# Residual kept in SBUF past the token norm, head 1's weights by slot, last head's states stored by ScalarE, low-rank columns beside head 0's values

## The chip, the cores and the metric

The kernel runs on one core of one Trainium2 chip. The metric is the device time of one execution in microseconds. All arithmetic is in fp32. "Record" below is one instruction in the trace; an fp32 matmul of the program makes two of them on TensorE (PE).

## The reference, cut to what matters

Two layers of a streaming encoder over 1024 prompt frames and 32 sample frames (NTOK = 1056 rows of D = 1024 features), with 256 memory rows:

```
h = rms_norm(x, g0)                                  # layer 0
u, a, b, zA, qB, kB, vB, zB = split(h @ W0)
o_A = gated_deltanet(silu(causal_conv(u)), a, b)     # 8 heads, 128x128 states
o_B = band_attention(qB, kB, vB)                     # 16 heads of 64
x += concat(rms_norm(o_A) * silu(zA), o_B * silu(zB)) @ Wout0
x += memory_attend(rms_norm(x), keys/values from rms_norm(mem))
h = rms_norm(x, g1)                                  # layer 1
q, k, v, lr, z = split(h @ W1)                       # lr has 16 columns
lg = log_sigmoid(lr @ W_gate_up + gate_bias) / 16
x += (rms_norm(gla(q, k, v, lg)) * silu(z)) @ Wout1
x += memory_attend(rms_norm(x), ...)
```

Outputs are x, the new states of both recurrences, the last convolution rows and the keys and values. The memory's keys and values of both layers are computed inside the GDN part.

## The kernel before, in words

The program is a series of stages, each with blocks in which the five engines run their own lists of instructions. A block ends when all engines have ended their lists, and the next begins after a barrier (recorded at L45, or at a block's own line such as L1834). Features lie on the 128 partitions: `hT` holds the normed input as 8 slabs of 128 features by 1056 tokens. `Wb` holds four weight slots of 1024x128. A projection of one head is cut into **jobs**: 352 tokens by 8 slabs, 16 records at L490 (GDN) or L1995 (GLA).

`turn_input` (L86 to L198) makes `hT`. For each of 9 tiles of 128 tokens (the last has 32) PE transposes the rows into PSUM (`turn_TP`, L138), ScalarE (ACT) copies them to `xT` (L160) and squares them into `sq` (L162), PE sums the squares with a matrix of ones (L128), ACT makes the reciprocal root, and VectorE (DVE) multiplies by gain and root into `hT`, 8 instructions per tile (L185). SyncE's queue (SP) loads the rows, the gain `g` (L115) and GDN's first weights (L59), then stores `xT` to `x_features` tile by tile (L119) and waits for these stores before the block ends. The residual is read back from `x_features` much later.

`gdn` (L205): PE's order at its start is head 0's first 3 jobs, gate columns (L675), 6 jobs, transposes of memory tile 0 (`turn_mem`, L668), 3 jobs, memory tile 1, then 36 transposes of 8 columns (L693, "tok"), then `head(0)`: 12 steps of head 1's projection as filler (24 records, L490) and the turn of conv k (L546). DVE copies tok (L1082), makes the decay differences (L903), prepares the parameters, and runs conv k and conv q (L938, L941), before which it copies the convolution's tails (L931, L932) and for that waits for the head's last projection copy (`proj_out` 12). ACT applies SiLU to conv k (L759, L760). SP loads head h+1's four weight slots in `head(h)`; for head 0 this stands after the wait for the stores of the turned memory (`m_st`), L364. After the last head SP loads band's first weights (L59, slots in the order of `ahead`), stores the last head's state, sample state and output rows (L372 to L387) and waits for them.

`band` (L1230) projects k first; PE and ACT wait at the start for constants (`consts`, two memsets of `Qz` by DVE, L1756). `EARLY_ORDER` and `BAND_COL` say which weight slot holds what.

`gla` (L1808) opens with a block of its own (L1834 to L1865): weights `wlr` of the 16 low-rank columns are loaded, PE multiplies them with `hT` (L1849), DVE copies the result to `lrT`, SP waits for the parameters. Then the main block starts: z0, z1, v, q, k of head 0 (`PLAN`), with 9 tiles of v at 256 columns (L1991).

Of the kernel before, what the change touches and what calls it, by code (L numbers as in the profile page):

```python
# [6 lines left out]
F32 = mybir.dt.float32  # L7
ACT = mybir.ActivationFunctionType
ALU = mybir.AluOpType
# [76 lines left out]
def turn_input(nc, ident, ones, eps, x_in, xT_dram, gain, hT, ahead):  # L86

    with ExitStack() as ctx:
        def sb(n, shape):
# [5 lines left out]
        xT = sb("xT", [128, KD, NTOK])  # L95
# [7 lines left out]
        turned, copied, squared, summed, rooted, rs_ok, h_out, st = (sem("turned"), sem("copied"), sem("squared"), sem("summed"),  # L103
                                                                     sem("rooted"), sem("rs_ok"), sem("h_out"), sem("st"))
# [4 lines left out]
        with nc.Block() as block:  # L109
            @block.sync  # L110
            def _(sp):
# [3 lines left out]
                sp.dma_start(g[:, :], gain.rearrange("(k p) -> p k", p=128), allow_slow_non_contiguous=True).then_inc(g_ld, 16)  # L115
# [29 lines left out]
            def _(act):  # L145
                act.preload_act_table_set("natural_log_exp_and_others")
# [10 lines left out]
                for t in range(TILES):  # L157
# [3 lines left out]
                    wait(act, summed, t - 1)  # L161
                    act.activation(sq[:, t % 2, :, 0:r], TP[:, t % 2, :, 0:r], ACT.Square).then_inc(squared, 1)  # L162
# [5 lines left out]
            def _(pool):  # L168
# [3 lines left out]
                                   base=0, pattern=[[-1, 128]], channel_multiplier=1).then_inc(ident_ok, 1)  # L172

# [31 lines left out]
def gdn(nc, ident, ones, eps, hT, W, w_ld, w_in, conv_w, conv_state, a_log, dt_bias, onorm_g, state_in,  # L205
        gate_rows, o_dram, conv_p, conv_s, state_p, state_s, mem, mem_layers, mem_T, ahead):
# [3 lines left out]
    with ExitStack() as ctx:  # L210
# [36 lines left out]
        OI = sb("OI", [128, TILES, 128])  # L247
# [112 lines left out]
        with nc.Block() as block:  # L360
            @block.sync
            def _(sp):
# [26 lines left out]
                def head(h, before):  # L389

                    for p, j in enumerate(ORDER):

                        sp.wait_ge(proj_done, h * 12 + 3 * p + 3)
                        load_w(h + 1, j, h * 128 + 128 + COL[j])
# [2745 lines left out]
```

## Time and profile before

| | |
|---|---|
| median of 3 runs | 3653.94 us (3649.12 to 3654.18) |
| the profiled execution | 3648.23 us, span 3646.5 us |
| mean granted TensorE clock | 0.985 |
| PE busy | 3506.4 us, 96% of the span |
| DVE, ACT, POOL busy | 1169.9, 1102.5, 514.8 us |
| read and written in HBM | 158.49 and 45.99 MB |

The span is the time from the first to the last instruction. A row of the timeline is a run of like instructions on one engine, with its start in us from the span's start, its length, their count, and in brackets the idle time ahead of it with what ended it. SPq is SP's list of DMA issues. A row of stretches gives busy time per engine and PEclk, the share of TensorE's full clock that was granted.

### The profile page before, as it was taken

The numbers are of one execution on the slowest core, as the hardware profiler recorded it, in microseconds if no ns is written. First come the engines' busy times: TensorE is split into PE (matmuls) and PEld (weight loads), VectorE is DVE, ScalarE is ACT, GpSimd is POOL, SyncE is SP. The second block draws the span as 40 slices with busy tenths as digits, with TensorE's granted clock in tenths as the row PEclk, the third lists the DMA queues.
The fourth block names the chain that finished last, engine by engine and source line by source line (L and its number), as shares of the span: only waits on it lengthen the run. The fifth ranks groups of instructions, "written<-read, shape, count | busy, mean of one in ns | idle before, by whom it ended". The sixth has DMA issues, their size and how long they took to land. (4 is left out here: it accounts for less than half of the span.)

```text
span 3646.5 us, 47398 instructions
## 1 busy us (share of the span) xinstructions
PE 3506.4 (96%) x16670; PEld 2579.1 (71%) x16670; DVE 1169.9 (32%) x2993; ACT 1102.5 (30%) x2794; POOL 514.8 (14%) x518
## 2 busy tenths in 40 slices
PE   7899999999799999999999998999999999899999
PEld 5577777777468777777766675677777777566676
DVE  2355555555213333333320234022221122220223
ACT  3333333333133443443310242022222222210242
POOL 0344444444000000000001002000000000011000
PEclk9899999999899999999999999999999999999999
DMA  5211311102412231222261102111111111371101
GB/s 138 64 32 32 26 35 31 37 26 94 95 42 45 40 31 42 45 46 82 96 196 47 35 10 75 41 29 39 50 44 43 29 43 38 109 234 46 35 1 48
DMA packets 254233, 206.85 MB, mean 57 GB/s; under 512 B 21071, under 2 KB 232175, under 8 KB 254039
## 3 DMA queue, kind: packets, MB, share of 16 engines
q1 hardware_dynamic: 249726, 194.83, 21.0%
q10 hardware_dynamic: 4320, 9.67, 0.7%
q8 instruction: 100, 1.64, 0.2%
q14 instruction: 87, 0.71, 0.1%
HBM read 158.49 MB, written 45.99 MB: 56 GB/s over the span
## 5 line engine op out<-in xcount | busy, mean ns | idle before, releaser
L490 PE MATMUL gdn_pj<-hT,Wb 128*128 128x352 f32 x1536 | 517.8, 463 | 28.8 <-PEq L45 15.8
L1995 PE MATMUL gla_pj<-hT,Wb 128*128 128x352 f32 x1536 | 470.0, 460 | 2.2 <-PEq L1834 1.6
L1426 PE MATMUL band_pj<-hT,Wb 128*128 128x384 f32 (+1 forms) x1152 | 385.1, 464 | 23.2 <-DVE band_tick L1761 20.2
L1995 PEld LDWEIGHTS gla_pj<-hT,Wb 128*128 128x128 f32 x1536 | 290.7, 190 | 151.0 <-issue 2.9
L490 PEld LDWEIGHTS gdn_pj<-hT,Wb 128*128 128x128 f32 x1536 | 267.6, 193 | 118.5 <-issue 32.6
L1426 PEld LDWEIGHTS band_pj<-hT,Wb 128*128 128x128 f32 x1152 | 206.6, 192 | 105.0 <-DVE band_tick L1761 20.5
L1991 PE MATMUL gla_pj<-gla_Wv,hT 128*128 128x256 f32 x1152 | 264.9, 379 | 0.0
L1991 PEld LDWEIGHTS gla_pj<-gla_Wv,hT 128*128 128x128 f32 x1152 | 217.7, 190 | 29.5
L1611 ACT ACTIVATE band_E<-band_NS,band_nm 128x576 f32<-128x576 f32 (+9 forms) x136 | 89.7, 660 | 213.8 <-DVE band_nm L1688 213.7
L1189 POOL TENSOR_TENSOR gdn_BT<-gdn_AT,gdn_level 128x384 f32<-128x384 f32 x144 | 143.8, 1029 | 35.3 <-DVE gdn_TT L972 17.9
L1456 PE MATMUL band_pj<-Wb,hT 128*128 128x128 f32 x1152 | 144.2, 276 | 0.0
L1519 PEld LDWEIGHTS band_PX<-band_ET,band_VT 128*128 128x128 f32 x976 | 127.1, 192 | 20.2
L1456 PEld LDWEIGHTS band_pj<-Wb,hT 128*128 128x128 f32 x1152 | 136.6, 192 | 0.7
L1519 PE MATMUL band_PX<-band_ET,band_VT 128*128 128x128 f32 x976 | 131.0, 275 | 0.0
L1688 DVE CUSTOM_DVE_ANT_0 band_NS<-band_SC,band_bias 128x576 f32<-128x576 f32 (+9 forms) x136 | 83.2, 611 | 138.8 <-issue 138.0
L2685 PE MATMUL fin_ps<-fin_R,fin_Wx 128*128 128x384 f32 (+1 forms) x384 | 123.1, 463 | 2.2 <-DVE fin_xT L2976 2.1
L2676 PE MATMUL fin_ps<-hT,Wb 128*128 128x384 f32 (+1 forms) x384 | 124.9, 460 | 0.0
L1489 PE MATMUL band_SC<-band_KN,band_Qz 128*128 128x288 f32 (+3 forms) x448 | 114.9, 374 | 3.5 <-issue 3.5
L2649 PE MATMUL fin_ps<-hT,fin_Wq 128*128 128x384 f32 (+1 forms) x384 | 117.2, 460 | 0.0
L2617 PE MATMUL fin_ps<-hT,Wb 128*128 128x384 f32 (+1 forms) x384 | 115.9, 460 | 0.0
L1621 ACT ACTIVATE band_ET<-band_PT 128x512 f32<-128x512 f32 (+3 forms) x136 | 70.7, 520 | 148.9 <-PE band_PX L1499 89.7
L2939 DVE TENSOR_TENSOR fin_xT<-fin_xT,fin_ps 128x384 f32<-128x384 f32 (+1 forms) x48 | 24.8, 521 | 279.3 <-PE fin_ps L2617 244.0
(412 smaller groups left out, 5419.3 us busy)
## 6 DMA issues: line engine op xcount, KB each, us to landing
Wb<-in_l_w_in_dram SPq DMA_DIRECT2D x96, 512.0 KB, 6.2
fin_xT<-x_features SPq DMA_DIRECT2D x16, 528.0 KB, 7.4
fin_R<-o_features SPq DMA_DIRECT2D x16, 528.0 KB, 9.7
Wb<-in_l_w_mkv_dram SPq DMA_DIRECT2D x8, 1024.0 KB, 5.5
Wb<-in_l_w_out_dram SPq DMA_DIRECT2D x16, 512.0 KB, 4.2
gla_Wv<-in_l_w_in_dram SPq DMA_DIRECT2D x8, 1024.0 KB, 5.2
o_features<-gla_OF ACTq DMA_DIRECT2D x14, 528.0 KB, 5.7
gdn_GB<-gate_rows SPq DMA_DIRECT2D x8, 544.0 KB, 3.6
```

The costliest lines, as they stand in the source:

```text
L490: mm = pe.matmul(pj[:, m % 2, 0:w], W[:, j, k, :], hT[:, k, c0:c0 + w], start=k == 0, stop=k == KD - 1)
L1189: pool.tensor_tensor(g3(BT, g), g3(AT, g), mask, ALU.mult).then_inc(masked, 1)
L1426: mm = pe.matmul(out[:, 0:w], W[:, j, k, :], hT[:, k, c0:c0 + w], start=k == 0, stop=k == KD - 1)
L1456: mm = pe.matmul(out[:, 0:128], hT[:, k, 128 * i:128 * i + 128], W[:, 3, k, :], start=k == 0, stop=k == KD - 1)
L1489: mm = pe.matmul(out[:, b, 0:w], q, KN[p][:, k0 + w * b:k0 + w * b + w], start=True, stop=True)
L1519: mm = pe.matmul(PX[:, 1, :], v, ET[:, u % 2, 128 * b:128 * b + 128], start=b == 0, stop=b == blocks(u) - 1)
L1991: mm = pe.matmul(pj[:, m % 2, 0:DV_C], hT[:, k, 128 * x:128 * x + 128], Wv[:, k, :], start=k == 0, stop=k == KD - 1)
L1995: mm = pe.matmul(pj[:, m % 2, 0:w], W[:, SLOT[kind], k, :], hT[:, k, c0:c0 + w], start=k == 0, stop=k == KD - 1)
L2617: mm = pe.matmul(ps[:, 3 * (n % 2) + c, 0:w], weights, src[:, c0:c0 + w], start=i == 0, stop=i == len(tiles) - 1)
L2649: mm = pe.matmul(ps[:, i % 3, 0:w], Wqt[:, h, k, :], hT[:, k, c0:c0 + w], start=k == 0, stop=k == KD - 1)
L2676: mm = pe.matmul(out[:, 0:w], Wz[:, x, k, :], hT[:, k, c0:c0 + w], start=k == 0, stop=k == KD - 1)
L2685: mm = pe.matmul(out[:, 0:w], Wo[:, k, 128 * x:128 * x + 128], O[:, k, c0:c0 + w], start=k == 0, stop=k == M_H - 1)
```

## The change

In `turn_input` `xT` becomes `x_kept`, a tile that lives through `gdn`; its nine stores and the wait for them are gone. The gain is loaded by ACT's queue. The squares are made by GpSimd (POOL) from SBUF, and PE's transposes wait for the copy and no longer for the square.

```diff
-                for t in range(TILES):
-                    sp.wait_ge(copied, t + 1)
-                    sp.dma_start(xT_dram.rearrange("(k p) t -> p k t", p=128)[:, :, cols(t)], xT[:, :, cols(t)]).then_inc(st, 16)
-                sp.wait_ge(st, TILES * 16)
...
-                    wait(pe, squared, t - 1)
+                    wait(pe, copied, t - 1)
...
+                act.dma_start(g[:, :], gain.rearrange("(k p) -> p k", p=128), allow_slow_non_contiguous=True).then_inc(g_ld, 16)
...
-                    act.activation(sq[:, t % 2, :, 0:r], TP[:, t % 2, :, 0:r], ACT.Square).then_inc(squared, 1)
...
+                    pool.tensor_tensor(sq[:, t % 2, :, 0:rows(t)], xT[:, :, cols(t)], xT[:, :, cols(t)], ALU.mult).then_inc(squared, 1)
```

In `gdn` SP stores `x_kept` as eight DMAs at the start; `dec`, `TM`, `BT`, `VV`, `KR`, `KE`, `OI` and `zs` become slices of `x_kept`, so ACT and DVE wait for `x_st` before they first write there. Head 1's weights are loaded one slot at a time (`next_w`). The memory transposes use two PSUM banks, and PE's order is changed. Conv k waits for `proj_out` 9, and the two tail copies stand between conv k and conv q.

```diff
+                for k in range(KD):
+                    sp.dma_start(xT_dram[128 * k:128 * k + 128, :], xT[:, k, 0:NTOK]).then_inc(x_st, 16)
                 sp.dma_start(sall[:, :, :], state_in.rearrange("h d v -> d h v")).then_inc(ld_state, 16)
+                next_w(0, 0)
+                next_w(0, 1)
...
-                        wait(pe, m_ok, 4 * m + 2 * r)
+                        wait(pe, m_ok, 2 * (2 * m + r - 1))
...
-                            mm = pe.transpose(X3[:, 2, 128 * k:128 * k + 128], M[m][:, c:c + 128], ident[:, :])
+                            mm = pe.transpose(X3[:, 2 - r, 128 * k:128 * k + 128], M[m][:, c:c + 128], ident[:, :])
...
+                act.wait_ge(x_st, KD * 16)
...
-                    dve.wait_ge(proj_out, h * 12 + 12)
...
+                    dve.wait_ge(proj_out, h * 12 + 9)
...
+                        if x == 1:
+                            wait(dve, v_turn, h * 4)
+                            dve.wait_ge(proj_out, h * 12 + 12)
```

At the end of `gdn` ACT issues the last head's four stores, output columns 0 to 767 as soon as they are ready; SP no longer does. Band's weights sit in other slots (`BAND_SLOT`), k's and q's are loaded first, and `EARLY_ORDER` follows. In `band` PE waits for `consts` after the k jobs, ACT before the first q norm.

```diff
-                        load_ahead(sp, [ahead[j] for j in ((2, 3) if x == 6 else (0, 1))])
+                        load_ahead(sp, [ahead[j] for j in ((0, 1) if x == 6 else (2, 3))])
...
-                store_state(H_A - 1)
-                store_out(H_A - 1)
...
+                act.wait_ge(s_ok, H_A * N)
+                act.dma_start(state_p[last:H_A, :, :].rearrange("o d v -> d (o v)"), S[:, 0, :]).then_inc(st_p, 16)
+                act.dma_start(state_s[last:H_A, :, :].rearrange("o d v -> d (o v)"), Sn[:, :]).then_inc(st_s, 16)
+                act.wait_ge(o_fin, last * 3 + 2)
+                act.dma_start(o_dram[128 * last:128 * H_A, 0:768], OF[:, 0:768]).then_inc(st_o, 16)
...
-BAND_COL = [4112, 5136, 7184, 6160]
...
+BAND_SLOT = [2, 3, 0, 1]
...
-                pe.wait_ge(consts, 2)
-                for _ in stream(0, 0):
-                    pass
+                for m, _ in enumerate(stream(0, 0)):
+                    if m + 1 == ends[place["k", 0]]:
+                        pe.wait_ge(consts, 2)
```

In `gla` the opening block is gone. The 16 low-rank columns are appended to head 0's v weights, whose 9 tiles become 272 columns wide; ACT copies them apart (9 small copies), PE transposes them (`turn_lr`, 9 transposes) after z1, and DVE makes `lrT`. Head 0's order is z0, v, z1, q, k.

```diff
-                            mm = pe.matmul(pl[:, c, 0:w], wlr[:, k, :], hT[:, k, c0:c0 + w], start=k == 0, stop=k == KD - 1)
...
+        Wv = sb("Wv", [128, KD, DV_C + RANK])
...
+        PLAN0 = PLAN[0:3] + PLAN[6:15] + PLAN[3:6] + PLAN[15:]
...
+                sp.dma_start(Wv[:, :, DV_C:DV_C + RANK], w_cols[:, :, COL["lr"]:COL["lr"] + RANK]).then_inc(lr_ld, 16)
...
+                            act.activation(lr[:, x, :], pj[:, m % 2, DV_C:DV_C + RANK], ACT.Copy)
```

How the instructions move, at three places. PE's list at the start of `gdn` (`gdn_AT` and `gdn_QK` are the two memory tiles, `gdn_WQ`, `gdn_EG`, `gdn_OF` the rows of tok, the last x12 the head start's filler); a count here is of the program's matmuls, two records each, before:

```order
24 L490 MATMUL gdn_pj<-hT,Wb 128x352 x48
25 L668 MATMUL gdn_X<-ident,gdn_AT 128x128 x8
26 L490 MATMUL gdn_pj<-hT,Wb 128x352 x24
27 L668 MATMUL gdn_X<-ident,gdn_QK 128x128 x8
28 L693 MATMUL gdn_X<-ident,gdn_WQ 128x8 x18
29 L693 MATMUL gdn_X<-ident,gdn_EG 128x8 x9
30 L693 MATMUL gdn_X<-ident,gdn_OF 128x8 x9
31 L490 MATMUL gdn_pj<-hT,Wb 128x352 x12
32 L546 MATMUL gdn_X<-ident,gdn_act 128x128 x9
```

and in the change:

```order
24 L497 MATMUL gdn_pj<-hT,Wb 128x352 x48
25 L675 MATMUL gdn_X<-ident,gdn_AT 128x128 x8
26 L497 MATMUL gdn_pj<-hT,Wb 128x352 x8
27 L675 MATMUL gdn_X<-ident,gdn_QK 128x128 x8
28 L497 MATMUL gdn_pj<-hT,Wb 128x352 x8
29 L701 MATMUL gdn_X<-ident,gdn_WQ 128x8 x18
30 L701 MATMUL gdn_X<-ident,gdn_EG 128x8 x9
31 L701 MATMUL gdn_X<-ident,gdn_OF 128x8 x9
32 L497 MATMUL gdn_pj<-hT,Wb 128x352 x20
33 L553 MATMUL gdn_X<-ident,gdn_act 128x128 x9
```

One job now stands between the memory tiles, one between tile 1 and tok, and one joins the filler behind tok. SP's queue at the same place (`Wb` there is head 1's weights), before:

```order
18 L416 DMA gdn_sall<-in_state_l_gdn_dram 128x8x128
19 L418 DMA gate_rows<-gdn_WQ 8x1152
20 L367 DMA gdn_GB<-gate_rows 128x1088
21 L425 DMA mem_features<-gdn_BT 128x8x128
22 L425 DMA mem_features<-gdn_VV 128x8x128
23 L425 DMA mem_features<-gdn_KR 128x8x128
24 L425 DMA mem_features<-gdn_KE 128x8x128
25 L364 DMA Wb<-in_l_w_in_dram 128x8x128 x4
```

and in the change:

```order
15 L420 DMA x_features<-x_kept 128x1056 x8
16 L421 DMA gdn_sall<-in_state_l_gdn_dram 128x8x128
17 L361 DMA Wb<-in_l_w_in_dram 128x8x128 x2
18 L425 DMA gate_rows<-gdn_WQ 8x1152
19 L364 DMA gdn_GB<-gate_rows 128x1088
20 L361 DMA Wb<-in_l_w_in_dram 128x8x128
21 L433 DMA mem_features<-x_kept 128x8x128 x4
22 L361 DMA Wb<-in_l_w_in_dram 128x8x128
```

Three of head 1's four slots are now issued ahead of the memory's stores. SP's queue at the end of `gdn` (`gdn_S`, `gdn_Sn` the states, `gdn_OF` the output rows, `band_rel` band's first load), before:

```order
93 L458 DMA out_dram<-gdn_U 128x512 x2
94 L59 DMA Wb<-in_l_w_in_dram 128x8x128 x2
95 L372 DMA out_dram<-gdn_S 128x128
96 L373 DMA out_dram<-gdn_Sn 128x128
97 L386 DMA o_features<-gdn_OF 128x1024
98 L387 DMA o_features<-gdn_OF 128x32
99 L360 UNCONDITIONAL_BRANCH
100 L1331 UNCONDITIONAL_BRANCH
101 L1379 DMA band_rel<-in_l_b_rel_bias_dram 16x257
```

and in the change:

```order
90 L467 DMA out_dram<-gdn_U 128x512 x2
91 L59 DMA Wb<-in_l_w_in_dram 128x8x128 x2
92 L357 UNCONDITIONAL_BRANCH
93 L1354 UNCONDITIONAL_BRANCH
94 L1402 DMA band_rel<-in_l_b_rel_bias_dram 16x257
```

The four stores have gone to ACT's list, behind its last instruction there.

## Rows read from the trace of the kernel before

**Rows 1.** The page's part 1, busy us and share of the span

```profile
PE 3506.4 (96%) x16670; PEld 2579.1 (71%) x16670; DVE 1169.9 (32%) x2993; ACT 1102.5 (30%) x2794; POOL 514.8 (14%) x518
```

**Rows 2.** What PE waited for, whole run: us in total, times, longest

```profile
PE gdn_X L546 <- ACT gdn_act L760: 7.4, 6, 1.5
```

**Rows 3.** PE timeline, input stage: start, us, line, out<-in, xcount, [idle before <-releaser]

```profile
16.65 1.95 PE L128 MATMUL turn_PS<-turn_sq,ones 128*128 128x128 f32 x16
...
48.03 16.31 PE L490 MATMUL gdn_pj<-hT,Wb 128*128 128x352 f32 x48 [15.79 <-PEq L45]
```

**Rows 4.** DVE and SP's queue, timeline, input stage

```profile
15.70 12.69 DVE L185 SCALAR_TENSOR_TENSOR hT<-turn_xT,turn_g,turn_rs 128x128 f32<-128x128 f32 x48 [13.80 <-DMA turn_g<-in_l_norm_g_dram]
...
31.38 3.49 DVE L185 SCALAR_TENSOR_TENSOR hT<-turn_xT,turn_g,turn_rs 128x128 f32<-128x128 f32 x16 [0.37 <-ACT turn_rs L154]
...
21.44 21.98 SPq L119 DMA_DIRECT2D x_features<-turn_xT  x9
```

**Rows 5.** DVE and POOL timelines, GLA around 2397, GDN at 99.61

```profile
2397.68 2.00 DVE L2246 TENSOR_TENSOR gla_KK<-gla_raw,gla_E 128x32 f32<-128x32 f32 x1
...
2396.71 2.92 POOL L2320 TENSOR_TENSOR gla_QS<-gla_QG,gla_FC 128x1088 f32<-128x1088 f32 x1 [106.98 <-DVE gla_QG L2243]
...
99.61 2.11 POOL L1154 TENSOR_TENSOR gdn_conv<-gdn_conv,gdn_tap 128x1091 f32<-128x1091 f32 x1
```

**Rows 6.** Stretches: us, busy PE, PEld, DVE, ACT, POOL, PEclk, DMA, GB/s

```profile
36.00:40.00 4.00, 0.00 (x0) 0.00 (x0) 0.00 (x0) 0.00 (x0) 0.00 (x0) 0.50 1.06 297
```

**Rows 7.** PE timeline, start of GDN

```profile
108.84 0.60 PE L668 MATMUL gdn_X<-ident,gdn_AT 128*128 128x128 f32 x4
...
111.42 14.37 PE L490 MATMUL gdn_pj<-hT,Wb 128*128 128x352 f32 x48
...
129.74 0.94 PE L693 MATMUL gdn_X<-ident,gdn_WQ 8*128 8x8 f32 x15 [1.47 <-DVE gdn_KE L1076]
...
145.50 9.96 PE L490 MATMUL gdn_pj<-hT,Wb 128*128 128x352 f32 x24 [12.98 <-issue]
```

**Rows 8.** DVE, ACT and SP's queue, timeline, start of GDN

```profile
90.60 1.06 ACT L864 ACTIVATE gdn_BT<-gdn_AT 128x1024 f32<-128x1024 f32 x1
...
132.55 0.28 DVE L1082 COPY gdn_tok<-gdn_X 128x72 f32<-128x72 f32 x1 [2.96 <-PE gdn_X L693]
...
142.94 1.06 ACT L759 ACTIVATE gdn_act<-gdn_conv 128x1024 f32<-128x1024 f32 x1
...
138.44 7.85 SPq L364 DMA_DIRECT2D Wb<-in_l_w_in_dram  x4
```

**Rows 9.** DVE timeline, border of two heads of GDN

```profile
351.50 0.16 DVE L931 COPY gdn_tails<-gdn_U 128x9 f32<-128x9 f32 x1
```

**Rows 10.** PE, SP's queue and POOL, timeline, end of GDN, start of band

```profile
992.66 19.66 PE L1426 MATMUL band_pj<-hT,Wb 128*128 128x384 f32 x57 [20.22 <-DVE band_tick L1761]
...
970.08 1.20 SPq L59 DMA_DIRECT2D Wb<-in_l_w_in_dram  x2
...
980.87 0.43 SPq L387 DMA_DIRECT2D o_features<-gdn_OF  x1
...
987.34 0.20 POOL L1772 MEMSET band_pair_ones<- 128x128 f32 x1 [15.50 <-POOLq L45]
```

**Rows 11.** DMA issues from 969 to 993: xcount, KB each, us to landing

```profile
Wb<-in_l_w_in_dram SPq DMA_DIRECT2D x2, 512.0 KB, 11.6
...
o_features<-gdn_OF SPq DMA_DIRECT2D x1, 16.0 KB, 4.9
```

**Rows 12.** PE and POOL, timeline, start of GLA

```profile
2271.02 15.78 PE L1849 MATMUL gla_pl<-hT,gla_wlr 128*16 128x512 f32 x48 [8.36 <-DMA gla_wlr<-in_l_w_in_dram]
...
2288.39 28.64 PE L1995 MATMUL gla_pj<-hT,Wb 128*128 128x352 f32 x96 [1.58 <-PEq L1834]
...
2316.86 31.24 PE L1991 MATMUL gla_pj<-gla_Wv,hT 128*128 128x256 f32 x144
...
2268.52 1.01 POOL L1859 MEMSET gla_fresh<- 128x1088 f32 x1 [6.73 <-POOLq L45]
```

More of the change, by code:

```diff
@@ L83, with turn_input @@
 MEM, M_H, M_D = 256, 4, 128
-def turn_input(nc, ident, ones, eps, x_in, xT_dram, gain, hT, ahead):
+def turn_input(nc, ident, ones, eps, x_in, xT, gain, hT, ahead):
     with ExitStack() as ctx:
@@ L172, in _ @@
                                    base=0, pattern=[[-1, 128]], channel_multiplier=1).then_inc(ident_ok, 1)
+                for t in range(TILES):
+                    pool.wait_ge(copied, t + 1)
+                    wait(pool, summed, t - 1)
+                    pool.tensor_tensor(sq[:, t % 2, :, 0:rows(t)], xT[:, :, cols(t)], xT[:, :, cols(t)], ALU.mult).then_inc(squared, 1)
             @block.vector
@@ L387, in store_out, with next_w, head, next_inputs @@
                     sp.dma_start(o_dram[ds(h * 128, 128), NP:NTOK], OF[:, NP:NTOK]).then_inc(st_o, 16)
[L389 to L394, printed above, removed]
-                    if before:
-                        store_state(h - 1)
-                        store_out(h - 1)
+                def next_w(h, p):
+                    sp.wait_ge(proj_done, h * 12 + 3 * p + 3)
+                    load_w(h + 1, ORDER[p], h * 128 + 128 + COL[ORDER[p]])
+                def head(h):
+                    for p in range(4):
+                        next_w(h, p)
+                    store_state(h - 1)
+                    store_out(h - 1)
+                    next_inputs(h)
+                def next_inputs(h):
                     sp.wait_ge(eg_ok, h + 1)
@@ L655, in _, with first_tile @@
                 first = project(0)
-                def first_tile():
-                    for _ in range(24):
+                def first_tile(steps=24):
+                    for _ in range(steps):
                         next(first, None)
@@ L1425, in stream @@
                             for k in range(KD):
-                                mm = pe.matmul(out[:, 0:w], W[:, j, k, :], hT[:, k, c0:c0 + w], start=k == 0, stop=k == KD - 1)
+                                mm = pe.matmul(out[:, 0:w], W[:, BAND_SLOT[j], k, :], hT[:, k, c0:c0 + w], start=k == 0, stop=k == KD - 1)
                                 if k == KD - 1:
@@ L2088, in head, with turn_lr @@
                     turn_out(2)
-                for _ in project(0):
-                    pass
+                def turn_lr():
+                    pe.wait_ge(proj_out, V0_END)
+                    for c, (c0, w) in enumerate(BANKS):
+                        for a in range(0, w, 128):
+                            r = min(128, w - a)
+                            t = (c0 + a) // 128
+                            mm = pe.transpose(X[0:RANK, c, a:a + r], lr[0:r, t, :], ident[0:r, 0:r])
+                    mm.then_inc(lr_turn, 1)
+                for i, _ in enumerate(project(0, PLAN0)):
+                    if i + 1 == KD * Z0_END:
+                        turn_lr()
                 head(0, True)
```

162 lines of the change are left out of this document (82 added, 80 removed).

## The prediction

> **What bounds the kernel now.** First the page's busy shares: PE works 3506.4 of 3646.5 us [rows 1], so all that a change off PE's list can win is some 140 us of gaps. Next the view of what PE waited for, where the gaps are few and long; at the border of GDN's heads it has 7.4 us in six pieces [rows 2], and PE's timeline shows the others in place: 15.79 us at the end of the input stage [rows 3], 12.98 before head 1's first job [rows 7], 20.22 before band's first projection [rows 10] and 8.36 before the low-rank matmuls [rows 12]. The change touches each of these five. So I go through PE's timeline place by place and ask where PE starts again; what other engines do between counts only through that. The clock is the third thing to see: in the long gap of the input stage PEclk stands at 0.50 [rows 6], the lower of its two levels (1.2 of 2.4 GHz), and the 48 records after that gap take 16.31 us [rows 3] where 48 of the same kind take 14.37 with no gap ahead [rows 7]. A gap thus costs itself and some 1.9 us behind it, as long as it is long enough for the clock to fall.
>
> **Input stage.** Before, DVE ends at 34.87 (31.38 + 3.49), SP still issues stores until 43.42 (21.44 + 21.98) [rows 4] and PE begins GDN at 48.03 [rows 3]. The nine stores go; what is late next is the chain through POOL's squares. A square is 1024 elements per partition: by 2.11 us for 1091 [rows 5] it takes 1.98. DVE's eight multiplications of a tile take 12.69/6 = 2.12 us [rows 4], and they read two inputs from SBUF. Can both run at once? Rows 5 say no: a DVE multiplication of 32 elements takes 2.00 us and ends at 2399.68, when POOL's neighbour, begun at 2396.71, ends (2399.63), and POOL's 1088 elements took 2.92 instead of about 2.1. I take them as taking turns: 8 x (1.98 + 2.12) + some 1.7 for the tile of 32 = 34.5 us. The first copy ends at about 7.6, since PE's and ACT's first steps do not change, so DVE ends near 42.1; with some 0.5 of hand-overs and 1.3 of border (at the end of GDN one took 1.5, below) PE starts at 43.9. **Saved 4.1 us.** The gain no longer matters: it was waited for until 15.70 [rows 4], and DVE cannot begin before two squares and a root, at about 12. The gap still drops the clock, as before.
>
> The Trainium skill ("SBUF — State Buffer", section "Who interferes with whom") says the same as a rule: a DVE instruction with two SBUF inputs and a GpSimd instruction that reads SBUF hold a shared port exclusively, and one fully blocks the other. It speaks against this move of the squares. By it the sum is the one below; without it, PE would start at about 37.3 and the sum would be 6.6 us more.
>
> **Start of GDN.** From 108.84 to the end of head 1's first 24 records at 155.46 (145.50 + 9.96) [rows 7] PE needs 46.6 us. The work in it: eight memory transposes twice, at 0.60 per four some 2.2; three jobs 14.37; tok 2.8 (129.74 to DVE's 132.55 [rows 8]); 24 records at full clock 7.2 (half of 14.37). Together 26.6 us. The rest is waiting: for the single PSUM bank twice (from 109.44 to 111.42 with 0.6 of work, so 1.4 each), for DVE before tok 1.47, the 12.98, and 2.8 of low clock in the last 24 records. The 12.98 is head 1's weights: SP issued them from 138.44 [rows 8], behind the landing of the memory's stores. By slot, slots 0 and 1 follow head 0's jobs 3 and 6, long before. Is SiLU of conv k late instead? It ended at about 144.1 (142.94 + 1.06, then 0.24), 11.6 us after tok's copy [rows 8]. In the new order tok ends 2.2 + 9.6 + 2.8 = 14.6 us after 108.84's counterpart, so SiLU is ready at 26.2, PE at 26.6. That is a tie, where other heads wait 7.4/6 = 1.2 us [rows 2]; I take 0.6 for it. **Saved 19.4 us** (16 to 21). The eight stores of the residual (4.3 MB, 22 us of issue before) go out from about 45 and hold back ACT's first write into `x_kept`, at 90.60 before [rows 8] and 4 us earlier now: hidden, with over 15 us to spare, if issue and landing again take 25. Behind them on SP's queue stand head 1's slots and the gates' rows; `next_w(0, 1)` now waits for job 6, about 7 us past the old issue of the gate rows, which DVE needs only after tok, 25 us on: nothing. If that cover were gone, each microsecond late would be one on conv k. ACT gives up 9 squares, nothing waits for them.
>
> **Head border.** Conv k of the later heads ends the 7.4 us of waits [rows 2]. Two copies of 0.16 [rows 9] move behind it, 0.2 us per head with the issue. `proj_out` 9 comes earlier than 12, but DVE is not ready before. Six heads: **saved 1.2 us** (0 to 2.4).
>
> **End of GDN.** PE ends at 972.44 and begins band at 992.66 [rows 10]. Two pieces: the block starts at 987.34, and `consts` holds PE for another 5.3. The second goes entirely, since k's weights are now the pair loaded first. It would not without the new slots: the pair issued at 970.08 [rows 10] takes 11.6 us to land [rows 11]. The first: the last store is issued at 980.87, lands 4.9 later at 985.8, and the block begins 1.5 after that. ACT is free at about 971 and issues all four by 973. They then share the DMA engines with 1 MB of weights in flight. Between landing at once (973 + 4.9, less than which no row shows) and landing last, with the weights at 981.9, I take 979.9, nearer the first, since 0.65 MB of stores is less than the weights. PE restarts at 981.4. **Saved 11.2 us** (7 to 14; the low end has the stores held until 984). The Trainium skill ("DMA: Bandwidth & Descriptors", section "Issuing engines are not separate DMA queues") warns that a second issuing engine saves only the time of issue, as both use the same 16 engines; a strict reading puts the landing at the weights' 981.9 and the saving at 9.2, 2.0 less in the sum.
>
> **Start of GLA.** PE begins z0 at 2288.39; the opening block, which goes, has POOL start at 2268.52 [rows 12]. The 48 matmul records, the wait for `wlr` and the second border go, so z0 begins at 2268.6: 19.8. To be given back: z0 now runs at the low clock, 1.9 as after the input stage (the low-rank matmuls paid this before); 144 v records 16 columns wider, by (14.37/48 - 31.24/144)/96 = 0.86 ns per column [rows 7, 12] 144 x 13.8 ns = 2.0; nine transposes 1.0. ACT's nine small copies lie beside v tiles of 3.5 us each, and Wv has 14 us of z0 to land. **Saved 14.9 us** (13 to 16).
>
> **Sum.** 4.1 + 19.4 + 1.2 + 11.2 + 14.9 = 50.8 us. From the profiled execution 3648.23 - 50.8 = 3597.4. That execution lies 5.7 below the median of the runs shown, 3653.94, and against this median the forecast is 3653.94 - 50.8 = **3603.1 us**. The bounds of the terms, added, give 33 to 64 us.
>
> **Rivals.**
> 1. *POOL and DVE do overlap in the input stage.* For it: rows 5 show one pair only, with other shapes. Then PE's tiles bind as before, DVE ends some 1 us after its old 34.87 [rows 4], GDN starts near 37.3: 57.4 saved, 3596.5. Chance 0.10.
> 2. *The input stage slows PE.* PE has a 1.95 us piece per tile [rows 3] and eight transposes, some 0.9 by the four in 0.60 of rows 7; in a cycle of 4.1 us it stands idle a third of the time. If PEclk falls there to the 0.50 of rows 6, a tile costs some 5.3 us of PE (the two overlap a little) and the stage ends some 9 us later than I say, near 53: 41.8 saved, 3612.1. Against it: after pauses of 1.4 us the 48 records of rows 7 still ran at full clock. Chance 0.12.
> 3. *New waits eat part of starts and ends.* Conv k's chain, not PE, sets L546 (SiLU after other ACT work, or a clock that falls at tok's small transposes: 4 us), and the stores land after the weights (4 us): 42.8 saved, 3611. Chance 0.18.
> 4. *Slower.* DVE's tail copies now stand between conv k and conv q in every head, and wait for `v_turn` and `proj_out` 12. If these came late, conv q, its SiLU and all that is queued behind on DVE would shift. It decides from about 8.3 us per head over seven heads (50.8 + 7.3 over 7); but both now come before conv k begins. Chance 0.02, time 3661 or more.
> 5. *The freed time is off the path*: PE's long gaps close but turn up again at the next wait. PE at 96% speaks against it. 3650, chance 0.02.
>
> My forecast has the remaining 0.56. The range reaches over rivals 1 to 3 and the terms' bounds but not their sum on either end: **3589 to 3619**. A measurement of this kernel tells 0.2%, 7.3 us, from no change; faster by more has 0.96, within 0.02, slower 0.02.
>
> **What would show it.** In the changed profile: PE's first GDN record near 43.9, DVE's multiplications in runs of about 2.1 us with gaps of 2, and POOL's squares between them. No stores of `x_features` before that, eight after. The turn of conv k within 27 us of the first memory transpose, and head 1's weights issued before the memory's stores. Band's first record within 10 us of GDN's last; z0 right behind the border with 272-column tiles after it. Wrong would be: squares of 1.98 us beside DVE at 0.26 per multiplication, PEclk under 1.00 in the input stage, a wait on `x_st` on ACT, or conv q late behind the tails.

## The result and the profile after

| | before | the change |
|---|---|---|
| median of 4 runs | 3654.06 us (3649.12 to 3654.39) | 3609.08 us (3606.97 to 3610.31) |
| ratio, 95% interval | | 0.9883 (0.9872 to 0.9895) |
| the profiled execution | 3648.23 us, span 3646.5 | 3610.31 us, span 3608.6 |

The change wins 45.0 us by the medians, against a forecast of 50.8, and lies inside the range given. The two profiled executions are only 37.9 us apart, because that of before lay 5.8 us under its median and that of the change 1.2 above. The forecast was made in stages, so here are the stages, from PE's timeline in the two traces. A stage is the time between two marks, in us:

| stage (its first and last mark) | before | change | won | forecast |
|---|---|---|---|---|
| input stage, to GDN's first record | 48.03 | 49.17 | -1.1 | 4.1 |
| to the first memory transpose | 60.81 | 61.91 | -1.1 | 0 |
| to the turn of head 0's conv k | 46.46 | 25.14 | 21.3 | 19.4 |
| to GDN's last record | 817.14 | 817.67 | -0.5 | 1.2 |
| to band's first record | 20.22 | 13.84 | 6.4 | 11.2 |
| to the last record ahead of GLA | 1270.00 | 1273.02 | -3.0 | 0 |
| to GLA's z0 | 25.73 | 5.89 | 19.8 | 19.8 |
| to the end | 1358.11 | 1361.96 | -3.9 | -4.9 |

Some of these rows hold little more than scatter. In the traces of the runs below, stages whose code is that of the change vary by themselves: the input stage from 46.71 to 49.27 us (eight traces), GDN's heads from 816.7 to 817.8, band to GLA from 1268.6 to 1273.3, z0 to the end from 1361.2 to 1367.0. So the input stage lies between 1.2 us slower and 1.3 us faster than before, and the -3.0 and the close hit of -3.9 against -4.9 are within what one trace can be off.

The input stage is where the sum went most wrong. These are rows of POOL's, DVE's and PE's timelines in the changed kernel (start, us, engine, line, out<-in, count, idle time before and its end):

```profile
15.95 1.92 POOL L169 TENSOR_TENSOR turn_sq<-x_kept 128x1024 f32<-128x1024 f32 x1 [3.84 <-ACT x_kept L155]
...
29.18 6.26 POOL L169 TENSOR_TENSOR turn_sq<-x_kept 128x1024 f32<-128x1024 f32 x1 [2.47 <-ACT x_kept L155]
...
16.03 1.98 DVE L182 SCALAR_TENSOR_TENSOR hT<-x_kept,turn_g,turn_rs 128x128 f32<-128x128 f32 x1
...
14.45 19.24 DVE L182 SCALAR_TENSOR_TENSOR hT<-x_kept,turn_g,turn_rs 128x128 f32<-128x128 f32 x48 [12.54 <-ACT turn_rs L149]
...
35.49 3.78 PE L122 MATMUL turn_PS<-turn_sq,ones 128*128 128x128 f32 x16 [5.80 <-POOL turn_sq L169]
...
40.20 6.00 PE L122 MATMUL turn_PS<-turn_sq,ones 128*128 128x128 f32 x32
49.17 17.41 PE L497 MATMUL gdn_pj<-hT,Wb 128*128 128x352 f32 x48 [2.97 <-PEq L45]
```

Four squares begin amid DVE's run of 48 multiplications, at 15.95, 18.61, 21.98 and 24.67, and take 1.92 to 2.05 us each; the next multiplication then takes 1.98 us instead of 0.34 (the row at 16.03), because it waits for the square. The fifth square takes 6.26 us. It begins at 29.18, while DVE works through its multiplications without a break until 33.69, and ends 1.75 us after them. DVE's 48 multiplications, the four that waited among them, take 19.24 us instead of 12.69 [rows 4]. PE waits 5.80 us for that square, and the same 16 records that take 1.95 us at full clock [rows 3] take 3.78 after it. In the rows of stretches (busy time of PE, PEld, DVE, ACT and POOL, then PEclk, DMA and GB/s) the clock is at its lower level there, as in [rows 6], but now with PE at work:

```profile
32.00:36.00 4.00, 0.51 (x2) 0.51 (x3) 1.69 (x7) 0.00 (x0) 4.00 (x2) 0.84 0.01 2
36.00:40.00 4.00, 4.00 (x24) 3.77 (x22) 0.00 (x0) 0.65 (x2) 1.29 (x1) 0.50 0.00 0
40.00:44.00 4.00, 4.00 (x21) 3.94 (x21) 2.55 (x8) 0.41 (x2) 0.71 (x1) 0.50 0.01 2
```

The start of GDN went as forecast. PE's timeline there, answering to [rows 7]: no gap from the first memory transpose to conv k's turn, 40 records in 12.10 us at full clock, and L553 starts 25.14 us after 111.08.

```profile
111.08 1.04 PE L675 MATMUL gdn_X<-ident,gdn_AT 128*128 128x128 f32 x8
...
124.28 12.10 PE L497 MATMUL gdn_pj<-hT,Wb 128*128 128x352 f32 x40
136.22 1.15 PE L553 MATMUL gdn_X<-ident,gdn_act 128*128 128x128 f32 x9
```

At the end of GDN (PE, ACT's queue and the DMA issues with their KB and us to landing, answering to [rows 10, 11]) PE does start with the block, but the block starts late. The two stores of output rows took 9.4 and 9.2 us to land, and ACT needed from 952.18 to 959.30, 7.1 us, only to issue its four stores:

```profile
967.73 22.39 PE L1449 MATMUL band_pj<-hT,Wb 128*128 128x384 f32 x64 [13.85 <-PEq L45]
...
952.57 1.72 ACTq L904 DMA_DIRECT2D out_dram<-gdn_Sn  x1
954.32 2.56 ACTq L906 DMA_DIRECT2D o_features<-gdn_OF  x1
956.92 2.38 ACTq L908 DMA_DIRECT2D o_features<-gdn_OF  x1
...
Wb<-in_l_w_in_dram SPq DMA_DIRECT2D x2, 512.0 KB, 11.6
...
o_features<-gdn_OF ACTq DMA_DIRECT2D x1, 384.0 KB, 9.4
...
o_features<-gdn_OF ACTq DMA_DIRECT2D x1, 144.0 KB, 9.2
```

GLA's start (PE's timeline, answering to [rows 12]) is what was forecast: z0 at the low clock takes 16.07 us against 14.37, the wider v tiles 33.16 against 31.24, the nine transposes 1.16.

```profile
2246.64 16.07 PE L1999 MATMUL gla_pj<-hT,Wb 128*128 128x352 f32 x48 [5.89 <-PEq L45]
2262.55 33.16 PE L1995 MATMUL gla_pj<-gla_Wv,hT 128*128 128x272 f32 x144
...
2309.75 1.16 PE L2102 MATMUL gla_X<-ident,gla_lr 128*16 128x128 f32 x9
```

### The profile page after: what moved, and what is told of

It is laid out like the page before. It is cut to its first block and busy times, and to the rows that moved or that the text cites. A ratio compares the mean times of both kernels' runs of the same rounds, so it can differ in the third digit from the quotient of the medians.

```text
span 3608.6 us, 47321 instructions
## 1 busy us (share of the span) xinstructions
PE 3499.8 (97%) x16631; PEld 2577.4 (71%) x16631; DVE 1178.3 (33%) x2993; ACT 1095.7 (30%) x2794; POOL 533.1 (15%) x527
## 5 line engine op out<-in xcount | busy, mean ns | idle before, releaser
L1449 PE MATMUL band_pj<-hT,Wb 128*128 128x384 f32 (+1 forms) x1152 | 387.1, 465 | 16.8 <-PEq L45 13.8
L1995 PE MATMUL gla_pj<-gla_Wv,hT 128*128 128x256 f32 (+1 forms) x1152 | 266.8, 381 | 0.0
L1211 POOL TENSOR_TENSOR x_kept<-gdn_AT,gdn_level 128x384 f32<-128x384 f32 x144 | 144.2, 1032 | 35.8 <-DVE gdn_TT L993 18.5
L2705 PE MATMUL fin_ps<-hT,Wb 128*128 128x384 f32 (+1 forms) x384 | 124.8, 460 | 0.0
L3073 POOL TENSOR_TENSOR fin_acc<-fin_acc,fin_sq 128x384 f32<-128x384 f32 (+1 forms) x42 | 39.0, 929 | 532.2 <-ACT fin_sq L2822 532.0
L2354 POOL TENSOR_TENSOR gla_OR<-gla_OR,gla_rs 128x768 f32<-128x768 f32 x24 | 35.3, 1469 | 552.4 <-ACT gla_rs L2196 552.4
```

What stands on the lines that cost most here:

```text
L1211: pool.tensor_tensor(g3(BT, g), g3(AT, g), mask, ALU.mult).then_inc(masked, 1)
L1449: mm = pe.matmul(out[:, 0:w], W[:, BAND_SLOT[j], k, :], hT[:, k, c0:c0 + w], start=k == 0, stop=k == KD - 1)
L1995: mm = pe.matmul(pj[:, m % 2, 0:wv], hT[:, k, 128 * x:128 * x + 128], Wv[:, k, 0:wv], start=k == 0, stop=k == KD - 1)
L2705: mm = pe.matmul(out[:, 0:w], Wz[:, x, k, :], hT[:, k, c0:c0 + w], start=k == 0, stop=k == KD - 1)
```

## The experiments

Each starts from the changed kernel (3609.1 us) unless it says otherwise; stage times are read as in the table above.

**e1, the squares on ScalarE again.**

```diff
-                    wait(pe, copied, t - 1)
+                    wait(pe, squared, t - 1)
...
+                    wait(act, summed, t - 1)
+                    act.activation(sq[:, t % 2, :, 0:r], TP[:, t % 2, :, 0:r], ACT.Square).then_inc(squared, 1)
...
-                    pool.tensor_tensor(sq[:, t % 2, :, 0:rows(t)], xT[:, :, cols(t)], xT[:, :, cols(t)], ALU.mult).then_inc(squared, 1)
```

> The changed kernel with the squares back on ScalarE (read from PSUM), everything else kept, the early gain too. Theory A (the squares' place costs twice: POOL's square waits while DVE's two-input multiplications run, and PE's pause behind it drops the clock): DVE's multiplications take 0.26 us each again, PE's granted clock stays 1.00 to its last sum near 32 us, GDN's first record stands at 36 to 37 us instead of 49.17, and the time falls by 12 to 13 us to about 3597. Rival B (the stage is set by the loads of x or by the border): GDN begins at 44 or later and the time stays within 4 us of 3609.

Measured: 3595.06 us (3593.36 to 3597.43), ratio 0.9846 (0.9833 to 0.9860), 14.0 us below the change. DVE's and PE's timelines:

```profile
26.27 2.19 DVE L180 SCALAR_TENSOR_TENSOR hT<-x_kept,turn_g,turn_rs 128x128 f32<-128x128 f32 x8 [0.47 <-ACT turn_rs L149]
...
28.58 3.76 PE L122 MATMUL turn_PS<-turn_sq,ones 128*128 128x128 f32 x32
35.81 15.82 PE L495 MATMUL gdn_pj<-hT,Wb 128*128 128x352 f32 x48 [3.47 <-PEq L45]
```

DVE finishes each tile in 2.19 us and waits for the next, and GDN begins at 35.81. Theory A holds; B falls. Against the kernel before (48.03) the input stage is now 12.2 us shorter: so much the change wins there once the nine stores are gone and the squares have stayed on ScalarE.

**e2, a second set of squares on POOL that nothing reads**, on top of e1.

```diff
+                for t in range(TILES):
+                    pool.wait_ge(copied, t + 1)
+                    wait(pool, dummy, t)
+                    pool.tensor_tensor(junk[:, :, 0:rows(t)], xT[:, :, cols(t)], xT[:, :, cols(t)], ALU.mult).then_inc(dummy, 1)
```

> As the run before, plus POOL squaring each tile a second time into a tile that nothing reads. Theory A: PE and ACT do not wait for POOL, so PE's sums end near 32 us at full clock, but DVE's multiplications stretch to some 0.4 us beside POOL's squares and DVE ends at 41 to 43 us; GDN starts near 43 to 44, the time is about 7 us above the run before, near 3604; the 5 to 6 us that are left to the changed kernel's 49.17 are the clock and the sums' wait. Rival B (POOL and DVE do not exclude each other, POOL is only slow): DVE's multiplications stay at 0.26 us, GDN starts at 36 to 37 and the time is that of the run before.

Measured: 3601.97 us (3600.51 to 3604.25), ratio 0.9864 (0.9849 to 0.9879), 6.9 above e1. DVE's, POOL's and PE's timelines:

```profile
11.70 28.43 DVE L186 SCALAR_TENSOR_TENSOR hT<-x_kept,turn_g,turn_rs 128x128 f32<-128x128 f32 x72 [9.80 <-ACT turn_rs L151]
...
29.29 1.98 DVE L186 SCALAR_TENSOR_TENSOR hT<-x_kept,turn_g,turn_rs 128x128 f32<-128x128 f32 x1
...
22.75 8.36 POOL L173 TENSOR_TENSOR turn_junk<-x_kept 128x1024 f32<-128x1024 f32 x1 [2.73 <-ACT x_kept L157]
...
28.90 3.76 PE L124 MATMUL turn_PS<-turn_sq,ones 128*128 128x128 f32 x32
41.00 11.39 PE L501 MATMUL gdn_pj<-hT,Wb 128*128 128x352 f32 x30 [8.34 <-PEq L45]
```

No one waits for these squares, yet DVE's 72 multiplications take 28.43 us and one of the squares takes 8.36. PE's sums are untouched at full clock, and GDN begins 5.2 us later than in e1 (theory A had 7 to 8). So the two engines exclude each other, and that alone costs 5.2 of the 13.4 us between 35.81 and 49.17. The other 8.2 come only when PE's sums wait for the squares: the wait, and the low clock behind it. No run was made to take the two apart, but the trace of e7 (below) does it in part, since its input stage is that of the change. POOL's, PE's and the stretches' rows there:

```profile
29.16 6.26 POOL L169 TENSOR_TENSOR turn_sq<-x_kept 128x1024 f32<-128x1024 f32 x1 [2.20 <-ACT x_kept L155]
...
39.47 3.76 PE L122 MATMUL turn_PS<-turn_sq,ones 128*128 128x128 f32 x32
46.71 3.86 PE L495 MATMUL gdn_pj<-hT,Wb 128*128 128x352 f32 x6 [3.48 <-PEq L45]
...
40.00:44.00 4.00, 3.23 (x30) 3.12 (x28) 4.00 (x15) 1.19 (x4) 0.61 (x1) 1.00 0.01 2
```

The same square stands as long, but the clock is back at 1.00 by 40, where the changed kernel's trace has 0.50. The last 32 records take 3.76 us and not 6.00, and GDN begins at 46.71. So of the 8.2 us some 2.5 are the low clock, and they come and go between executions of the same code; the other 5.7 are the wait.

**e3, band's z and v weights issued behind the last output.**

```diff
                     if x >= 6:
+                        if x == 7:
+                            sp.wait_ge(o_fin, H_A * 3)
                         load_ahead(sp, [ahead[j] for j in ((0, 1) if x == 6 else (2, 3))])
```

> The changed kernel, but SyncE issues band's second pair of weights (z, v) only when the last head's output rows are done, so that ACT's four stores find free DMA engines. Theory A (the stores share the engines with 1 MB of weights, which made them land 9 to 12 us after issue): they land within 5 us, PE's gap between GDN and band falls from 13.85 to 7 to 8 us and the time by 6 us to about 3603. Rival B (the gap is ScalarE's slow issue and the landing's own latency): gap 12 or more, time 3608 to 3610. Rival C (the later weights now hold PE in band): the gap falls but PE waits for w_ld of z or v, time 3607 or more.

Measured: 3603.08 us (3598.33 to 3604.93), ratio 0.9863 (0.9848 to 0.9878), 6.0 below the change. ACT's queue, PE's timeline and the DMA issues:

```profile
950.40 0.44 ACTq L908 DMA_DIRECT2D o_features<-gdn_OF  x1
...
959.52 21.68 PE L1451 MATMUL band_pj<-hT,Wb 128*128 128x384 f32 x64 [8.30 <-PEq L45]
...
o_features<-gdn_OF ACTq DMA_DIRECT2D x1, 384.0 KB, 2.4
o_features<-gdn_OF ACTq DMA_DIRECT2D x1, 144.0 KB, 6.1
```

The same 384 KB land in 2.4 us instead of 9.4 once the weights are not in flight, their issue takes 0.44 us instead of 2.56, and the gap falls from 13.85 to 8.30. A holds in the main, with the gap 0.3 us over its 7 to 8: the 144 KB that go out together with the weights still take 6.1, where it said 5.

**e4, both.** Its edit is those of e1 and e3.

> Squares on ScalarE and band's z and v weights behind the stores, together. If both theories A hold the gains lie at different places and add: 12.5 + 6 us off the changed kernel, about 3590. If one falls, 3597 or 3603.

Measured: 3588.04 us (3587.32 to 3589.23), ratio 0.9825 (0.9811 to 0.9838). GDN begins at 36.47, band 8.21 us after GDN: the gains add, 21.0 us below the change against 20.0 for the two apart.

**e5, band's `consts` waits back at the start.** PE's and ACT's waits are placed as in the kernel before.

```diff
+                pe.wait_ge(consts, 2)
-                    if m + 1 == ends[place["k", 0]]:
-                        pe.wait_ge(consts, 2)
```

> The changed kernel with band's two waits for `consts` back at the start of PE's and ACT's lists. Theory A (PE bound, what is won at the start stays won): PE starts band 5.3 us after the block instead of with it, the gap grows from 13.85 to 19.1 us and the time by 5.3 us to about 3614.4. Rival B (PE's head start is given back at the next wait, for the first scores or the bias rows): the gap grows but a later wait of PE in band falls by the same, time within 2 us of 3609.

Measured: 3612.71 us (3611.62 to 3615.03), ratio 0.9896 (0.9879 to 0.9912), 3.6 above the change. PE's timeline:

```profile
972.21 21.24 PE L1449 MATMUL band_pj<-hT,Wb 128*128 128x384 f32 x64 [19.17 <-DVE band_tick L1784]
```

The gap grows by 5.3 us, but the first 64 records take 21.24 us instead of 22.39: begun later, they see less of the low clock. No later wait in band takes the gain back (up to the first scores the two run alike), so A holds with 1.2 us off; the rest of the difference to 3.6 is within the runs' scatter.

**e6, the last stores issued by SyncE again**, behind the weights.

```diff
                 sp.wait_ge(mk_st[1], 4 * 16)
+                store_state(H_A - 1)
+                store_out(H_A - 1)
...
-                act.dma_start(state_p[last:H_A, :, :].rearrange("o d v -> d (o v)"), S[:, 0, :]).then_inc(st_p, 16)
...
-                act.dma_start(o_dram[128 * last:128 * H_A, 0:768], OF[:, 0:768]).then_inc(st_o, 16)
```

> The changed kernel with the last head's four stores issued by SyncE again, behind the weights. Theory A (from run e3: what lands late is what shares the engines with the weights, whoever issues it): the block starts about 15 us after PE's last record, as before, against 13.85 now, so the time grows by 1 to 2 us only, 3610 to 3611. Rival B (my prediction's term: ScalarE's issue won 5.9 us): time about 3614 to 3615.

Measured: 3608.21 us (3607.26 to 3609.56), ratio 0.9883 (0.9866 to 0.9899): the change's own. PE's timeline:

```profile
966.41 8.81 PE L1443 MATMUL band_pj<-hT,Wb 128*128 128x384 f32 x19 [14.30 <-PEq L45]
```

The gap is 14.30 against 13.85. My term for ScalarE's issue, 5.9 us, is 0.4 us in the trace, and even that is not clear of scatter: in the six other traces that leave this place as in the change the gap is 13.73 to 14.18. B falls.

**e7, head 1's weights behind the memory's landing**, PE's new order kept.

```diff
-                next_w(0, 0)
-                next_w(0, 1)
...
-                next_w(0, 2)
...
-                next_w(0, 3)
                 sp.wait_ge(m_st, 64)
+                for p in range(4):
+                    next_w(0, p)
```

> The changed kernel with all four of head 1's slots loaded behind the landing of the memory's stores, PE's new order kept. Theory A (two causes shared the 12.98 us: the late weights and PE's order): the memory is ready some 118.5 us in, weights are issued near 127.5 and the first lands 7 us later at 134.5, where PE wants it at 129: a stall of 5 to 6 us, with the clock falling 7 to 8, time 3616 to 3617. Rival B (the weights alone were the 12.98): 13 us or more, 3622 and up. Rival C (the weights were never the wait, conv k's chain was): under 1 us, 3609 to 3610.

Measured: 3615.88 us (3614.44 to 3617.17), ratio 0.9905 (0.9888 to 0.9921), 6.8 above the change. PE's timeline and SP's queue:

```profile
133.77 9.15 PE L495 MATMUL gdn_pj<-hT,Wb 128*128 128x352 f32 x24 [7.26 <-DMA Wb<-in_l_w_in_dram]
...
125.86 8.45 SPq L361 DMA_DIRECT2D Wb<-in_l_w_in_dram  x4
```

PE waits 7.26 us by name for the weights, and the 24 records behind take 9.15 at the low clock where 7.2 are due. The stretch to the turn of conv k is 34.44 us: 9.3 more. A holds, with a stall some 2 us longer than worked out. The medians show less, 6.8, and the two traces only 4.1: in e7's the input stage is 2.5 us shorter and the stage from band to GLA 4.4, both with unchanged code.

**e8, the tail copies ahead of conv k again.**

```diff
-                    dve.wait_ge(proj_out, h * 12 + 9)
+                    wait(dve, v_turn, h * 4)
+                    dve.wait_ge(proj_out, h * 12 + 12)
+                    dve.tensor_copy(tv[:, 0, :, :], U[:, :, NP:NP + 3]).then_inc(tails_ok, 1)
+                    dve.tensor_copy(tv[:, 1, :, :], U[:, :, NP + 3 + NS:NP + 6 + NS]).then_inc(tails_ok, 1)
```

> The changed kernel with DVE's two tail copies ahead of conv k and the wait for proj_out 12 again. Theory A (what is on DVE just before conv k is its own result's latency, which the copies had covered): conv k starts at the same distance from the parameter copy L946 (0.38 us in the changed kernel) to 0.05, PE's wait at L553 stays 1.4 to 1.7 us per head, time 3608 to 3610. Rival B (my prediction's term): conv k 0.2 us later per head, PE's waits for SiLU up by 1.2 us in six heads, time 3610.3.

Measured: 3611.00 us (3607.34 to 3612.57), ratio 0.9887 (0.9871 to 0.9904), not to be told from the change by its time. DVE's timeline of e8, first head 0, then the border of two heads; below it the same border in the changed kernel:

```profile
127.88 0.17 DVE L946 COPY gdn_U<-gdn_cwc 128x6 f32<-128x6 f32 x1
129.53 0.16 DVE L950 COPY gdn_tails<-gdn_U 128x9 f32<-128x9 f32 x1 [1.48 <-ACT gdn_U L732]
...
334.13 0.17 DVE L946 COPY gdn_U<-gdn_cwc 128x6 f32<-128x6 f32 x1
...
334.56 0.79 DVE L957 TENSOR_SCALAR gdn_conv<-gdn_U,gdn_cwc 128x1091 f32<-128x1091 f32 x1
```

```profile
332.54 0.17 DVE L946 COPY gdn_U<-gdn_cwc 128x6 f32<-128x6 f32 x1
332.92 0.79 DVE L959 TENSOR_SCALAR gdn_conv<-gdn_U,gdn_cwc 128x1091 f32<-128x1091 f32 x1 [0.21 <-DVE gdn_U L946]
```

At a border conv k starts 0.43 us after L946 with the copies and 0.38 without: taking them away only lays bare the wait for L946's own result (0.21 us in the row above). Head 0 is another matter: there the copies wait 1.48 us for the last projection's copy, and its stretch grows from 25.14 to 26.54. A holds on DVE. On PE it is not the whole account: from head 0's turn of conv k to GDN's last record e8 needs 818.73 us against 817.67, and the ten other traces with the change's heads lie at 816.7 to 817.8. So the move may be worth another 1.1 us over the later heads; PE's waits there explain less than half of it, and the rest was not found. The time, 1.9 us above the change, allows either reading.

**e9, the whole GLA function of the kernel before.** The opening block is back (its central line):

```diff
+                            mm = pe.matmul(pl[:, c, 0:w], wlr[:, k, :], hT[:, k, c0:c0 + w], start=k == 0, stop=k == KD - 1)
```

> The changed kernel with the whole GLA function of the kernel before: the opening block with its own low-rank matmuls and its wait is back, head 0's v tiles are 256 wide. Theory A (the term as its stages show it: 19.8 us between the layers' border and z0, less 3.9 given back by the low clock, 16 more columns and nine transposes): PE's start of z0 moves from 5.9 to 25.7 us behind the layer before, the time to about 3625. Rival B (most is given back inside GLA, as a later wait grows): under 3617.

Measured: 3627.90 us (3622.70 to 3629.08), ratio 0.9933 (0.9918 to 0.9948), 18.8 above the change; its profiled span is 12.4 us longer. z0 stands 26.40 us behind the layer before and the rest takes 1355.28, so by the stages the term is 20.5 - 6.7 = 13.8 us:

```profile
2248.13 16.01 PE L1873 MATMUL gla_pl<-hT,gla_wlr 128*16 128x512 f32 x48 [8.80 <-DMA gla_wlr<-in_l_w_in_dram]
2265.72 28.64 PE L2019 MATMUL gla_pj<-hT,Wb 128*128 128x352 f32 x96 [1.58 <-PEq L1858]
```

A holds. The larger figure by the medians goes with a profiled execution (span 3621.0) that lies at the low end of its runs.

**e10, the weights behind the stores' landing**, on top of e4.

```diff
                         if x == 7:
-                            sp.wait_ge(o_fin, H_A * 3)
+                            sp.wait_ge(st_p, H_A * 16)
+                            sp.wait_ge(st_s, H_A * 16)
+                            sp.wait_ge(st_o, H_A * 32)
```

> Run e4 (squares on ScalarE, band's z and v weights behind the stores' issue), with SyncE issuing that pair only after the stores have landed. Theory A (in e3 the last store, 144 KB, still took 6.1 us beside the weights against 2.4 for the one before): all land within 2.5 us, the gap between GDN and band falls from 8.2 to 5.5 us, and the time from 3588.0 to 3585 to 3586. Rival B (the wait before the issue costs what the landing wins, or PE now waits for z or v): 3588 or more.

Measured: 3586.56 us (3584.42 to 3592.81), ratio 0.9821 (0.9808 to 0.9834), the fastest median of the study, though not told from e4 by it. All four stores land in 1.6 to 2.4 us and PE's gap falls from 8.21 to 5.20 us, as A has it (5.5):

```profile
o_features<-gdn_OF ACTq DMA_DIRECT2D x1, 384.0 KB, 2.4
...
o_features<-gdn_OF ACTq DMA_DIRECT2D x1, 144.0 KB, 1.8
```

**e11, PE's old order at the start of GDN**, weights by slot and both PSUM banks kept.

```diff
                 turn_mem(0)
-                first_tile(8)
+                first_tile()
                 turn_mem(1)
-                first_tile(8)
...
                 mm.then_inc(tok_done, 1)
-                first_tile(8)
```

> The changed kernel with PE's old order at the start of GDN (three jobs between the memory tiles, tok right behind tile 1, none behind it), head 1's weights by slot and the two PSUM banks kept. Theory A (conv k's chain of 11.6 us runs behind tok, and the filler must cover it): tok ends 18.3 us after the first memory transpose, SiLU of conv k 11.7 later, so the stretch to L553 is about 30 us instead of 25.14, time 3614. With run e7's 9.3 us the two account for most of the 21.3 us between 46.46 and 25.14. Rival B (order is worth nothing once the weights are early): 25 to 26 us, 3609 to 3610.

Measured: 3615.75 us (3613.65 to 3622.68), ratio 0.9905 (0.9890 to 0.9920), 6.7 above the change. The stretch is 32.94 us, 7.8 more. PE's timeline:

```profile
129.05 1.00 PE L700 MATMUL gdn_X<-ident,gdn_WQ 8*128 8x8 f32 x15 [2.23 <-DVE x_kept L1096]
...
131.83 9.61 PE L497 MATMUL gdn_pj<-hT,Wb 128*128 128x352 f32 x24
143.64 1.21 PE L553 MATMUL gdn_X<-ident,gdn_act 128*128 128x128 f32 x9 [2.21 <-ACT gdn_act L768]
```

PE waits 2.23 us for the turned memory ahead of tok, runs its filler at the low clock (9.61 for 24 records), and still waits 2.21 us for SiLU. A holds and undercounted: it had neither the wait ahead of tok nor the clock. The weights (9.3) and the order (7.8) make 17.1 of the 21.3 us won here; the second PSUM bank, and what the two hide of each other, are left for the other 4.2.

## Why the prediction was right, and where it was not

The total came out 5.8 us under the forecast by the medians, and inside a range that is 30 us wide. Stage by stage the traces miss by 12.9 us (37.9 against 50.8); the medians are kinder by 7.1 only because of which executions were profiled. Two of the five terms are wrong in their mechanism, below. So it was the size of the two right terms and the width of the range, and some luck, that made the total right. The range itself was not derived as it says: the terms' bounds as given add up to about 40 to 58 us, not 33 to 64, and the input stage, which missed most, had none.

**Right by the start of GDN and of GLA.** The two largest terms were 19.4 and 14.9 us. The traces have 21.3, and 19.8 less 3.9. e7 and e11 confirm both causes named for the first, e9 the second. The 0.6 us put aside for conv k's tie was not needed, because the turn of conv k waited for nothing in head 0. Part of it returned in the heads' stage: head 0 now waits 0.39 us for conv q, as the other heads do.

**Wrong in the input stage.** The step was that the two engines take turns, 8 x (1.98 + 2.12) us, so that DVE ends near 42.1. That they exclude each other was right (e2: 72 multiplications in 28.43 us in place of the 18.8 of e1, seven tiles of 2.19 and one run of 3.49). The rule of the Trainium skill ("SBUF — State Buffer", section "Who interferes with whom") agrees with these rows: while one works, the other stands. But neither the rule nor my sum says how long a square can stand. Four squares got in between two multiplications, and up to 33.69 DVE was ahead of my 4.1 us per tile, at 3.2. The fifth was passed over for 16 multiplications and ran only when DVE had nothing left. PE's sums hung on that square, PE paused 5.80 us and the clock fell. My rival on the clock had part of this outcome, but it had the pause spread over all tiles; it is one square near the end. Term: +4.1 forecast, -1.1 in the trace (-1.2 to +1.3 in eight), and 8.2 of the difference to e1 stand behind the sums' wait. That the gain no longer matters was right: in e1 DVE starts at 12.98 instead of 15.70 and ends at 34.97, against 34.87 before.

**Wrong at the end of GDN.** The step was a landing at 979.9, nearer to the free engines than to the weights, after an issue of all four stores in 2 us. The issue took 7.1 us, and the last store landed 9.2 us after its own began, at 966.1, which is 984.7 counted from GDN's end as in the forecast: 4.8 us late, and the whole miss of the term (6.4 for 11.2, under its lowest bound of 7). That is the second half of rival 3, stores that land behind the weights. Moving the issue to ScalarE was worth 0.4 us (e6), not 5.9. That agrees with the stricter sentence of the Trainium skill beside that step ("DMA: Bandwidth & Descriptors", section "Issuing engines are not separate DMA queues"), that a second issuing engine wins only the issue. What counted was what else was in flight (e3, e10). `consts` was the larger part, 5.3 us of gap and 4.1 with the clock (e5); that the new slots were its condition is argued in the prediction and was not tested.

**Head border.** 1.2 us was forecast as 0.2 per head, and the stage lost 0.5, outside the bounds of 0 to 2.4. On DVE e8 shows 0.05 us per head, not 0.2, and 1.4 in head 0; on PE the stage shows 1.1 more (e8). What the change adds in this stage, so that it is no shorter than before, stays open: PE waits for SiLU at the turn of conv k in five heads for 8.0 us, where before it was 7.4 in six [rows 2].

**Not in the sum.** From GDN's start to the first memory transpose the change loses 1.1 us, the same records at the low clock for longer (17.41 against 16.31). From band to GLA it loses 3.0: 0.5 in the first 64 records, most of the rest in short falls of the clock (below), which come and go from run to run: that stage is 1268.6 to 1273.3 us in the other twelve traces. In the medians the errors of -5.2 and -4.8 are partly covered by +1.9 at GDN's start and by scatter. Neither the slower rival nor the one of time off the path showed anything.

## What to carry to other kernels

Where one engine bounds a kernel by 96%, its few long gaps are most of what can be won; go through them one by one, and for each ask what is late next and whether the clock falls. Before moving elementwise work to GpSimd, look whether VectorE runs two-input instructions from SBUF at that time, and whether the bounding engine waits for the moved result: as a price on VectorE alone it was 5.2 us, with PE waiting for the result 11 to 13. Put a bound on how long one such instruction may stand, not only on the sum of both engines' work. At the end of a stage issue what must land before what can wait; who issued it mattered little here.

## What the runs showed of the hardware that was not expected

Which of the two engines stands is not settled by their exclusion. In each of the eight traces with the change's squares four squares got in between two multiplications of an unbroken run, after at most 0.2 us, and held the next multiplication for about 1.98 us; the fifth began just as they did, in the middle of a multiplication, and took 6.25 or 6.26 us, until VectorE had nothing more to do. In e2 one took 8.36 us and got in at 29.29, again between two multiplications. Why these and not the others stays open.

A DMA's issue is not free of what is in flight: the issue of the same 384 KB took ScalarE 2.56 us beside the weights and 0.44 us without them (e3).

The same pause does not always lower PE's clock. In band PE waits 1.88 us in the kernel before and 1.96 in the changed one, at the same point of the program. Before, the next six records take 2.16 us; in the change 3.85 us, with PEclk at 0.65 and 0.50 in the stretches of 2 us from 1338:

```profile
1362.60 0.43 PE L1489 MATMUL band_SC<-band_KN,band_Qz 128*128 128x64 f32 x2 [1.88 <-issue]
1362.87 2.16 PE L1426 MATMUL band_pj<-hT,Wb 128*128 128x384 f32 x6
```

```profile
1338.23 0.43 PE L1512 MATMUL band_SC<-band_KN,band_Qz 128*128 128x64 f32 x2 [1.96 <-issue]
1338.50 3.85 PE L1449 MATMUL band_pj<-hT,Wb 128*128 128x384 f32 x6
```

So it is in all traces: the pause is 1.9 to 2.4 us in each of the thirteen, and the six records take 3.5 to 3.9 us in four of them (the change, e2, e8, e9) and 2.2 in the nine others. e1 and e2 differ only in the input stage, 1300 us earlier; there the pauses are 1.97 and 2.00 us and the records take 2.15 and 3.85. The fall is thus not the work of this pause and its place in the program alone, and its cause stays open. It costs 1.7 us here. That such falls are a good part of the 3 to 6 us between runs of one kernel is argued, not shown.
